# Index scores in rounded parts on 128 rows, decay exponents on ScalarE, two modulation sets in the first network

## The reference

```python
mod = silu(c) @ w_ada + b_ada              # 9 chunks of 2048: the modulation
h = h + 0.5 * g1 * swiglu(mod(rms(h)))     # first network, width 5632
h = h + g2 * mixer(mod(rms(h)))            # 'hn @ w_in', then two branches
h = h + 0.5 * g3 * swiglu(mod(rms(h)))     # second network
# branch 1, state space: 8 groups of 4 heads, causal convolution, softplus dt
seg = acum[:, :, None] - acum[:, None, :]
y_diag = (cc @ bm.T) * exp(where(causal, seg, -inf)) @ x
# branch 2, attention over the 64 keys with the largest index score
rel = relu(einsum('bthd,bsd->bths', q_idx, k_idx))   # 16 heads of 64
score = einsum('bths,bth->bts', rel, w_idx) * idx_scale
```

## Time and profile before

| | us |
|---|---|
| median of 3 runs | 2491.59 |
| lowest, highest | 2489.63, 2493.53 |
| the profiled execution, its own time | 2491.51 |
| its span, first to last instruction | 2489.8 |

### The profile page before, as it was taken

The page is one execution under the profiler, slowest core; times in us unless marked ns, Lnnn a source line. Parts: engine busy times, 40 slices in busy tenths (PEclk is TensorE's granted clock), DMA queues, the critical chain, the costliest instruction groups (busy, mean ns, idle before and its releaser), DMA issues.

```text
span 2489.8 us, 33136 instructions
## 1 busy us (share of the span) xinstructions
PE 2459.8 (99%) x12083; PEld 2075.6 (83%) x12083; DVE 1893.2 (76%) x2168; ACT 1161.6 (47%) x1402; POOL 169.4 (7%) x273
## 2 busy tenths in 40 slices
PE   7999999999999999999999999999999999999999
PEld 5778888888888999898888888888888888888887
DVE  6886679898988989988987777777789555555556
ACT  4444444444446656645556444344544444444443
POOL 4210000000000001111100000000000000000000
PEclk9999999999999999999999999999999999999999
DMA  9975579999986889985544788796698766666665
GB/s 368 375 281 190 193 239 367 312 359 313 361 293 220 270 283 326 305 270 170 181 149 146 270 267 297 254 319 236 236 310 301 221 209 210 210 210 211 211 210 172
DMA packets 290613, 642.78 MB, mean 258 GB/s; under 512 B 26066, under 2 KB 26676, under 8 KB 289588
## 3 DMA queue, kind: packets, MB, share of 16 engines
q1 hardware_dynamic: 269600, 571.41, 67.9%
q0 software_dynamic: 19136, 65.05, 7.9%
q10 hardware_dynamic: 1748, 4.62, 0.5%
HBM read 622.59 MB, written 18.41 MB: 257 GB/s over the span
## 4 chain that ended last, share of the span: by engine, by line
PE 92%; DVE 4%; DMA 2%; ACT 1%; issue 1%; ACTq 0%; DVEq 0%
PE psum L2497 27%; PE psum L2499 27%; PE psum L2498 27%; PE psum L2797 3%; PE psum L2799 3%; PE psum L2798 3%; PE psum L2835 2%; PE psum L2485 1%; DVE w_lo L1541 1%; DMA raw<-in_ffn_w 1%; DVE score L2250 0%; DMA badas<-in_b_ada 0%; PE psum L2539 0%; ACT w_hi L1014 0%; PE psum L2578 0%
## 5 line engine op out<-in xcount | busy, mean ns | idle before, releaser
L1014 ACT ACTIVATE w_hi<-raw 128x1024 fp32r<-128x1024 f32 (+1 forms) x850 | 898.0, 1059 | 1034.0 <-PE psum L2499 819.2
L1541 DVE TENSOR_TENSOR w_lo<-raw,w_hi 128x1024 fp32r<-128x1024 f32 (+1 forms) x850 | 1033.5, 1220 | 448.9 <-ACT w_hi L1014 447.0
L2497 PE MATMUL psum<-w_hi,xT_hi 128*128 128x512 f32 x1984 | 777.6, 392 | 8.1 <-issue 5.4
L2498 PE MATMUL psum<-w_lo,xT_hi 128*128 128x512 f32 x1984 | 773.3, 390 | 0.0
L2499 PE MATMUL psum<-w_hi,xT_lo 128*128 128x512 f32 x1984 | 773.1, 390 | 0.0
L2497 PEld LDWEIGHTS psum<-w_hi,xT_hi 128*128 128x128 f32 x1984 | 373.1, 188 | 91.3 <-issue 14.2
L2499 PEld LDWEIGHTS psum<-w_hi,xT_lo 128*128 128x128 f32 x1984 | 373.0, 188 | 78.5
L2498 PEld LDWEIGHTS psum<-w_lo,xT_hi 128*128 128x128 f32 x1984 | 373.2, 188 | 75.2
L2497 PE MATMUL psum<-w_hi,aT_hi 128*128 128x512 f32 x704 | 274.7, 390 | 0.0
L2499 PE MATMUL psum<-w_hi,aT_lo 128*128 128x512 f32 x704 | 274.0, 389 | 0.0
L2498 PE MATMUL psum<-w_lo,aT_hi 128*128 128x512 f32 x704 | 273.9, 389 | 0.0
(11 more groups left out here) (305 smaller groups left out, 2116.3 us busy)
## 6 DMA issues: line engine op xcount, KB each, us to landing
raw<-in_ffn_w SPq DMA_DIRECT2D x528, 512.0 KB, 4.6
ada_raw<-in_w_ada SPq DMA_DIRECT2D x224, 512.0 KB, 6.3
raw<-in_w_in SPq DMA_DIRECT2D x224, 512.0 KB, 4.5
ada_raw<-in_w_ada POOLq DMA_DIRECT2D x32, 512.0 KB, 6.9
ada_more<-in_w_ada POOLq DMA_DIRECT2D x32, 512.0 KB, 7.4
raw<-in_w_br_ssd SPq DMA_DIRECT2D x32, 512.0 KB, 5.1
raw<-in_w_br_att SPq DMA_DIRECT2D x32, 512.0 KB, 4.6
raw<-in_w_out SPq DMA_DIRECT2D x32, 512.0 KB, 5.1
```

Of the source, the lines that this page charges most:

```text
L1014: nc.scalar.activation(w_hi[:, n.slot(SPLIT), 0:size], raw[:, n.slot(RAW), 0:size], ACT.Copy).then_inc(hi_ready, 1)
L1541: nc.vector.tensor_tensor(w_lo[:, n.slot(SPLIT), 0:size], raw[:, n.slot(RAW), 0:size], w_hi[:, n.slot(SPLIT), 0:size], ALU.subtract).then_ ...
L2497: nc.tensor.matmul(o, hi[:, kt + k, toks], whi, start=a, stop=False)
L2498: nc.tensor.matmul(o, hi[:, kt + k, toks], wlo, start=False, stop=False)
```

## The change

Queries and keys of the index are split into a rounded high and a low part. `qs[0]` holds even heads' high part on rows 0 to 63 and their low part on rows 64 to 127, `qs[1]` the odd heads' the other way round; a product is then two rounded ones on all 128 rows, against `kiT_hi` and `kiT_lo`. ScalarE writes the high parts, VectorE the low ones. The decay's exponents become relu(a - b) on ScalarE, with the exponential of minus that; `acum` loses its sign. Two modulation sets move from the mixer to the units from 43 on of the first network, and the one left in the mixer lies in its steps 40 to 71. `k_lo` moves one step ahead. Some semaphores are merged (`c_turned`, `c_ready`, `h_loaded`, `k_lo_ready`, `q_lo_ready`, `v_hi_ready` into neighbours, with their counts adjusted), and `fold_s` grows to 8 sets; those lines are left out here.

```diff
@@ -57,7 +57,7 @@
-ADA_PEELED = (0, 2)
+ADA_PEELED = (2, 2)
@@ -67,7 +67,7 @@
-ADA_MIXED = 3
+ADA_MIXED = 1
@@ -224,7 +224,9 @@
     cT = place("cT", at_temp + 60 * KB, [GROUPS, T])
-    qiT = place("qiT", at_temp + 68 * KB, [IDX_H // 2, T])
+    qs = (place("qs0", at_temp + 68 * KB, [IDX_H // 2, T], F32R), place("qs1", at_h, [IDX_H // 2, T], F32R))
+    kiT_hi = place("kiT_hi", at_temp + 12 * KB, [T], F32R)
+    kiT_lo = place("kiT_lo", at_temp + 13 * KB, [T], F32R)
     oT_hi = place("oT_hi", at_temp + 52 * KB, [KT, T], F32R)
@@ -674,7 +673,7 @@
 
-        return LATE[f] + (i * 5 // 4 if f == 0 else i * 5 // 3)
+        return LATE[f] + (i * 2 if f == 0 else i * 5 // 3)
 
@@ -694,7 +693,7 @@
                    for i in range(ADA_MIXED) for k in range(KT + ADA_COLS // FOLD_COLS)]
-    MIXED_AT = dict(zip([w for w in range(UPB + 6, 16 * UPB) if light(w)], MIXED_STEPS))
+    MIXED_AT = dict(zip([w for w in range(5 * UPB, 14 * UPB) if light(w)], MIXED_STEPS))
     assert len(MIXED_AT) == len(MIXED_STEPS)
@@ -796,7 +795,7 @@
                         if g >= 2:
-                            sp.wait_ge(seg_ready, g - 1)
+                            sp.wait_ge(seg_bent, g - 1)
                         sp.dma_start(cum_spread[:, g % 2], cum_dram[4 * g:4 * g + 4, :].rearrange("(o r) n -> o r n", o=1)
@@ -1323,17 +1322,22 @@
             act.wait_ge(unit_done, end[b])
-            for j in range(2):
-                ins = nc.scalar.activation(qiT[:, 4 * i + 2 * j:4 * i + 2 * j + 2, :],
-                                           psum[:, pair(b) + j, :].rearrange("p (k t) -> p k t", k=2), ACT.Copy)
-            ins.then_inc(pair_read[b % 2], 1)
+            for e in range(2):
+                own = slice(64 * e, 64 * e + 64)
+                ins = nc.scalar.activation(qs[e][own, 4 * i:4 * i + 4, :],
+                                           psum[own, pair(b):pair(b) + 2, :].rearrange("p b (k t) -> p (b k) t", k=2), ACT.Copy)
+            ins.then_inc(index_hi, 1)
+
+        def ki_out():
+            act.wait_ge(ada_used, ADA_MERGE * KT)
+            nc.scalar.activation(kiT_hi[:], kiT[:], ACT.Copy).then_inc(index_hi, 1)
 
...
@@ -1378,9 +1382,21 @@
 
+        def ssd_segments(g):
+
+            act.wait_ge(cum_in[g % 2], 16 * (g // 2 + 1))
+            act.wait_ge(acum_ready, 1)
+            if g:
+                act.wait_ge(y_raw, g)
+            for half in range(HALF):
+                for k in range(4):
+                    ins = nc.scalar.activation(decay[:, 2 * half, k, :], cum_spread[:, g % 2, k, half * P:(half + 1) * P],
+                                               ACT.Relu, scale=-1.0, bias=acum[:, half, 4 * g + k:4 * g + k + 1])
+            ins.then_inc(seg_bent, 1)
+
         def decay_exp(g):
-            act.wait_ge(seg_ready, g + 1)
-            nc.scalar.activation(decay[:, 0:3:2], decay[:, 0:3:2], ACT.Exp).then_inc(decay_ready, 1)
+            act.wait_ge(seg_bent, g + 1)
+            nc.scalar.activation(decay[:, 0:3:2], decay[:, 0:3:2], ACT.Exp, scale=-1.0).then_inc(decay_ready, 1)
 
@@ -1453,6 +1469,8 @@
                             qi_out(b)
+                            if WBLOCKS[b][1] == 0:
+                                ki_out()
                         if kind[b] == "v":
@@ -1474,6 +1492,8 @@
                     s = ssd_start[g]
+                    if n == s + 2:
+                        ssd_segments(g)
                     if n == s + 3:
@@ -1662,11 +1682,12 @@
                 e, k = divmod(peeled[f], KT)
+                second = e == ADA_PEELED[f] - 1
                 e += (ADA_FIRST, ADA_FFN2)[f]
                 ada_add(At(e * KT + k), k)
-                if e == N_ADA - 1 and 1 <= k <= ADA_COLS // FOLD_COLS:
+                if second and 1 <= k <= ADA_COLS // FOLD_COLS:
                     fold(At(e - 1), (k - 1,))
-                if e == N_ADA - 1 and k == KT - 1:
+                if second and k == KT - 1:
                     fold(At(e))
@@ -1852,6 +1873,7 @@
             sub_units(n + 1)
+            ada_peeled(0)
             if n - 3 == at_unit["w3", 0, 7]:
@@ -2111,28 +2133,20 @@
-            dt_do(nc.vector.tensor_scalar(acum[:, 0:2, :], psum[:, 4, 0:64].rearrange("p (s n) -> p s n", s=2),
-                                          -1.0, None, ALU.mult))
+            dt_do(nc.vector.tensor_copy(acum[:, 0:2, :], psum[:, 4, 0:64].rearrange("p (s n) -> p s n", s=2)))
...
-            nc.vector.tensor_tensor(acum[:, 2, :], psum[:, 4, 64:96], acum[:, 0, :], ALU.add).then_inc(acum_ready, 1)
+            nc.vector.tensor_tensor(acum[:, 2, :], psum[:, 4, 64:96], acum[:, 0, :], ALU.subtract).then_inc(acum_ready, 1)
...
-        def ssd_segments(g):
-
-
-            dve.wait_ge(cum_in[g % 2], 16 * (g // 2 + 1))
-            dve.wait_ge(acum_ready, 1)
+        def ssd_masks(g):
+
...
-            for half in range(HALF):
-                for k in range(4):
-                    nc.vector.tensor_scalar(decay[:, 2 * half, k, :], cum_spread[:, g % 2, k, half * P:(half + 1) * P],
-                                            acum[:, half, 4 * g + k:4 * g + k + 1], 0.0, ALU.add, ALU.min)
@@ -2214,27 +2228,41 @@
...
+
+        def qi_lo(b):
+            i = WBLOCKS[b][1]
+            dve.wait_ge(index_hi, (1, 3)[i])
+            for e in range(2):
+                own, other = slice(64 * e, 64 * e + 64), slice(64 - 64 * e, 128 - 64 * e)
+                ins = nc.vector.tensor_tensor(qs[e][other, 4 * i:4 * i + 4, :],
+                                              psum[own, pair(b):pair(b) + 2, :].rearrange("p b (k t) -> p (b k) t", k=2),
+                                              qs[e][own, 4 * i:4 * i + 4, :], ALU.subtract)
+            ins.then_inc(pair_read[b % 2], 1)
+
+        def ki_low():
+            dve.wait_ge(index_hi, 2)
+            nc.vector.tensor_tensor(kiT_lo[:], kiT[:], kiT_hi[:], ALU.subtract)
@@ -2379,6 +2407,10 @@
                         v_lo(b)
+                    if kind[b] == "qi" and n == end[b] + 3:
+                        qi_lo(b)
+                        if WBLOCKS[b][1] == 0:
+                            ki_low()
                 if n == FRONT_END + 5:
@@ -2390,7 +2422,7 @@
                     if n == s + 2:
-                        ssd_segments(g)
+                        ssd_masks(g)
                     if n == s + 4:
@@ -2409,7 +2441,6 @@
                     top_out()
-                if n == s + 15:
                     k_lo()
@@ -2871,13 +2902,13 @@
                 pe.wait_ge(pair_read[qb % 2], qb // 2 + 1)
-                pe.wait_ge(kiT_ready, 1)
             else:
...
                 for e in range(2):
-                    rows = slice(64 * e, 64 * e + 64)
-                    ins = plain(psum[:, 5 + e, half * T:(half + 1) * T], qiT[rows, j, half * P:(half + 1) * P], kiT[rows, :])
+                    o, both = psum[:, 5 + e, half * T:(half + 1) * T], qs[e][:, j, half * P:(half + 1) * P]
+                    plain(o, both, kiT_hi[:], True, False)
+                    ins = plain(o, both, kiT_lo[:], False, True)
             ins.then_inc(index_done, 1)
```

More of the change, by code:

```diff
@@ L176, in build @@
     dta = place("dta", region(HALF * SSD_H * 4), [HALF, SSD_H])
-    fold_s = place("fold_s", base[0], [6, ADA_COLS // FOLD])
+    fold_s = place("fold_s", base[0], [8, ADA_COLS // FOLD])
     sp_v = place("sp_v", region(HALF * SSD_H * 4), [HALF, SSD_H])
@@ L368, in build @@
     kiT_ready = sem("kiT_ready")
+    index_hi = sem("index_hi")
     dt_step = sem("dt_step")
@@ L381, in build @@
     seg_ready = sem("seg_ready")
+    seg_bent = sem("seg_bent")
     decay_ready = sem("decay_ready")
@@ L404, in build @@
     head_ready = sem("head_ready")
-    k_lo_ready = sem("k_lo_ready")
-    q_lo_ready = sem("q_lo_ready")
-    v_hi_ready = sem("v_hi_ready")
+    head_lo = sem("head_lo")
     p_lo_ready = sem("p_lo_ready")
@@ L989, in _ @@
         act.dma_start(c_row[0:KT, :], c[0].rearrange("(r n) -> r n", n=P)).then_inc(c_in, 16)
-        act.wait_ge(c_ready, 1)
+        act.wait_ge(cols_ready, 1)
         nc.scalar.activation(cact[:], vecT[:, 0:KT], ACT.Silu).then_inc(cact_ready, 1)
@@ L1335, in v_out @@
                 ins = nc.scalar.activation(vt_hi[:, half, :], psum[:, pair(b) + half, :], ACT.Copy)
-            ins.then_inc(v_hi_ready, 1)
+            ins.then_inc(head_ready, 1)
         def head_squares(i, b):
@@ L1520, in mixer @@
             merged_hi(mT2_hi, 0)
-            act.dma_start(h[:], h_dram).then_inc(h_loaded, 16)
+            act.dma_start(h[:], h_dram).then_inc(h_spilled, 16)
             cast_units(n + 6)
@@ L1607, in _ @@
         nc.vector.memset(fold_tmp[:], 0.0).then_inc(fold_step, 1)
-        dve.wait_ge(c_turned, 1)
-        nc.vector.tensor_copy(vecT[:, 0:KT], psum[:, 1, 0:KT]).then_inc(c_ready, 1)
+        dve.wait_ge(rows_turned, 1)
+        nc.vector.tensor_copy(vecT[:, 0:KT], psum[:, 1, 0:KT]).then_inc(cols_ready, 1)
         def columns():
-            dve.wait_ge(rows_turned, 1)
+            dve.wait_ge(rows_turned, 2)
```

(24 more changed lines are left out.)

3 lines of the change are left out of this document (removed).

## The result

The changed kernel took 2496.28 us (median of 18 runs, 2493.88 to 2501.56) beside 2491.40 for the kernel before (18 runs, 2488.94 to 2493.86). The ratio is 1.0024 with a 95% interval of 1.0018 to 1.0030, so it is slower by 4.5 to 7.5 us (the two medians alone are 4.9 apart). The forecast was 2496.2. The profiled execution has a span of 2493.7 us, 3.9 longer than before.

A forecast was written before the change was run, and what follows sets the result against it. TensorE was taken as the bound, busy in all but 30 us. From 2491.59: -2.4 (index) + 5.7 (wait) + 2.4 (clock) - 1.2 (late VectorE) + 0.1 (ScalarE) = +4.6, giving 2496.2 us, range 2492.5 to 2499.5.

The forecast's parts named there:

- The wait: Before the first index product near 1130, TensorE waits 5.7 us (5.0 to 6.6) for `qi_lo` from VectorE.
- The clock: Behind that wait the clock drops to its lower level and charges 2.4 us, bounds 0 and 3.5.
- rival 2: Same wait, but the low clock lasts longer than near the start; passes +5.0 once the clock costs 2.8; chance 0.41.
- The index steps: Eight index products on TensorE, each 0.95 us long, gain 0.31 a step, taken as 2.4 us in all.
- Late VectorE: TensorE's waits for VectorE's low parts at 1211 to 1221 shrink: gain 1.2 us (0 to 1.7), 0.5 left.
- the 1.73 us that was called the most to be had: Three late matmul starts at 1211.7, 1217.7 and 1221.0; moving VectorE work can give back 1.73 us and no more.
- the place at 826: Called the largest other place of the low parts' 2.7 us in five, behind twelve convolution steps the change leaves alone.
- The moved sets: Modulation sets moved from mixer to first network, about 175 to 345 us: cost nothing; if cover failed, 1 to 3 us.
- `k_lo` one step earlier change[s] no order that anyone waits for: Claim that the merged semaphores and the earlier `k_lo` make nobody wait; it had no term in the sum.
- the extra 0.1 that did not show: Term of +0.1 us in the sum for ScalarE's extra work elsewhere.
- rival 1: The forecast itself: wait and clock nearly paid for, time within 0.2% of the kernel before; chance 0.45.
- Rivals 3 and 4: 3: the clock doesn't fall, or hardly, 2493.8 us, chance 0.09. 4: the wait is hidden, 2488.0 us, chance 0.05.

The follow-up runs named there:

- e6b_lo_early: The changed kernel with the index queries' low part (`qi_lo`) one step earlier in VectorE's program: 2490.15 us, ratio 0.9999 to the kernel before.
- e2_no_relu: The changed kernel with the decay's exponents back on VectorE: 2495.64 us, ratio 1.0021 to the kernel before.
- e5b_kept_busy: The changed kernel with 26 matmuls that nobody reads ahead of the first index step's wait: 2494.65 us, ratio 1.0019 to the kernel before.
- e7b_k_back: The changed kernel with `k_lo` back at its old step and with its own semaphore: 2495.64 us, ratio 1.0021 to the kernel before.
- e4_sets_alone: The kernel before with only the two modulation sets moved to the first network: 2490.28 us, ratio 1.0003 to the kernel before.
- e8b_all_three: The changed kernel with `qi_lo` one step earlier, the first index step one unit later and `k_lo` back: 2488.19 us, ratio 0.9988 to the kernel before.
- e3_relu_alone: The kernel before with only the decay's exponents moved to ScalarE: 2489.61 us, ratio 0.9993 to the kernel before.

## Why the prediction was right

**The wait: mechanism and place right, 0.44 us too short.** Forecast 5.7, measured 6.14. The copies took 2.08 where 1.9 was counted, the relus 2.35 (2.3), the cast to `sub` 1.07 (1.10), `sub` and the two subtractions 3.72 (3.5), the signal 0.14 (0). One step of the count is added wrongly: 1132.2 + 3.5 is 1135.7, not 1135.8, so its own terms give a wait of 5.6 and a sum of +4.5. e6b_lo_early, which takes relus, cast and `sub` out of the chain, has 1.3 us of wait, and e2_no_relu, without the relus, 3.6: these three make most of it, not the subtractions. The relus' 0.29 us each was worked out from a spacing with a scalar column. The Trainium skill, "ScalarE: Activation LUTs", section "What ACT_TABLE_LOAD costs", has 280 ns and 0.833 ns a column for an instruction whose bias is a pointer operand, and an overlap of 93 ns where such instructions follow each other. The estimate from that page is 0.29 us as well, and the trace agrees with 2.35 / 8.

**The clock: 2.4 forecast, 2.06 measured (e5b_kept_busy against after).** It fell as forecast. The estimate took the stretch near the start for five microseconds, but those are only its part that lay on the units: before's granted clock is 0.50 there from 40.7 to 47.5, 6.8 us as well. So rival 2's condition, a low clock that lasts longer than near the start, did not come about; of the 6.8 us 2.4 ran out under the wait, which the prediction did not consider. e7b_k_back has 2.7 for the same stop.

**The index steps: 2.4 forecast, 2.40 measured.** From 1124 to 1190 the unit matmuls move by 5.80, and 6.14 + 2.06 - 5.80 = 2.40; 1.86 of it are the last six steps, 0.31 each. A step takes 0.95 us at full clock, as counted from the earlier trace rows.

**Late VectorE: 1.2 forecast, 1.36 measured.** But the stops were worth more than the 1.73 us that was called the most to be had. At each of the three places the matmul after the late one starts about 0.1 late too (the last at 1222.42, 0.34 behind 1222.08 instead of 0.23), as the prediction counted for the index step and not here: about 2.05 in all. 0.70 of it stayed, where 0.5 was forecast:

```profile
1224.53 0.39 PE L2530 MATMUL psum<-w_hi,xT_lo 128*128 128x512 f32 x1
1225.35 0.50 PE L2528 MATMUL psum<-w_hi,xT_hi 128*128 128x512 f32 x1 [0.44 <-DVE w_lo L1561]
1225.69 0.39 PE L2529 MATMUL psum<-w_lo,xT_hi 128*128 128x512 f32 x1
```

The prediction also misread where the 2.7 us of the earlier trace rows lie. 1.22 and 0.24 of them are idle time at 129.7 and 172, and the place at 826 is not among the five. The argument doesn't hang on it. e2_no_relu shows the other side: without the relus' move the index steps' gain is eaten there.

**The moved sets: nothing forecast, nothing measured** (e4_sets_alone, 0.2 us). VectorE was put at about 156 us busy between 175 and 345 and is at 147.7: durations of instructions that overlap a little had been added up. The DMA share was put at 0.91 and is 0.83.

**The step that failed: "`k_lo` one step earlier change[s] no order that anyone waits for".** It cost 0.95 us at 1236, shown by the changed kernel's wait and by its absence in e7b_k_back. VectorE does 2.3 us of work (`kT_lo` and the `sub` behind it) ahead of `qT_lo`, and TensorE's turns stand right behind that. e7b_k_back takes back the place and the merged signal together; the turns start 0.15 us behind the end of `qT_lo`, which is what they wait for in either kernel, so it is the place in VectorE's order that costs.

**The sum.** 6.14 + 2.06 - 2.40 - 1.36 + 0.95 = +5.4, and -0.3 in the rest of the span, gives the table's +5.1; forecast +4.6. The misses in the wait (+0.44) and `k_lo` (+0.95) were covered in part by the clock (-0.34), VectorE (-0.16), the extra 0.1 that did not show, and the -0.3. That the median came out within 0.1 us of the forecast is luck: the ratio allows 4.5 to 7.5 us, and misses of 0.4 and 0.95 were made up by others. Rivals 1 and 2 are one mechanism cut at 5 us, and the interval straddles that line; the clock's price, on which they were to differ, was rival 1's in the changed kernel's trace (2.06) and all but rival 2's in e7b_k_back's (2.7 of 2.8). Rivals 3 and 4 are out: the clock fell, and the wait was not hidden.

## What to carry to other kernels

A product made cheaper on the bounding engine is worth its saving only if its new operands are signalled in time: count from the block's end through every instruction ahead of the signal in each engine's order, those of other edits too, to the place where the bounding engine asks. A stop of several microseconds on TensorE can cost more than itself, because the matmuls behind it run at the lower clock (both stops of 6 us did, shorter ones did or didn't, last section); filling it, or better, moving the asker or the signal by one step, is a one-line edit. And any instruction moved within an engine's order is a term of the sum, however small it looks: one step earlier for `k_lo` cost as much as three index steps gained.

## What the runs showed of the hardware

The same stop of 5.99 us brought a low-clock stretch of about 6.8 us twice, but it began 2.4 us ahead of the end of the stop in one trace and 1.0 in the other, and cost 2.1 and 2.7 us. A stop of 3.65 us brought a stretch of 3.4; one of 1.31 brought none.

The length of a stop alone does not decide this. At the wait for `aT_lo`, 1.92 us in e8b_all_three were followed by 3.4 us of low clock, and 1.69 and 1.61 at the same place in e3_relu_alone and e7b_k_back by none:

```profile
452.30 0.59 PE L2530 MATMUL psum<-w_hi,aT_hi 128*128 128x512 f32 x1 [1.92 <-DVE aT_lo L1838]
...
453.54 0.63 PE L2530 MATMUL psum<-w_hi,aT_hi 128*128 128x512 f32 x1
453.97 0.63 PE L2531 MATMUL psum<-w_lo,aT_hi 128*128 128x512 f32 x1
```

Near 69.8 us e2_no_relu and e4_sets_alone both stop for 2.31 us at the same matmul. These are the windows behind it, first of e2_no_relu, then of e4_sets_alone, with 8 matmuls in the first and 14 in the second:

```profile
70.00:73.00 3.00, 3.00 (x8) 2.33 (x8) 1.54 (x3) 1.06 (x1) 0.72 (x1) 0.50 1.04 385
```

```profile
70.00:73.00 3.00, 3.00 (x14) 2.46 (x14) 1.52 (x3) 1.06 (x1) 0.72 (x1) 1.00 1.05 391
```

Behind the first 20 us, the longest stop without a fall is 2.76 us, in e3_relu_alone up to 144.2. So a stop of about 2 us may or may not bring the low clock, and nothing here says which it will be.

Copies of 64 partitions by 1024 columns took 1.02 us each (two in 2.05) and the subtractions 1.22, where instructions of 128 partitions by 1024 columns take 1.04 and 1.22: half the rows save nothing.

The stretch ahead of the index scatters. By the same matching the traces lie between 3.3 us ahead of before and 1.0 behind it at 195 us, and from 402 to 606 us e3_relu_alone and e7b_k_back lose a further 1.9 to 2.0 and e8b_all_three 3.8. The wait for `aT_lo` is 1.6 to 1.9 of it in each, and in e8b_all_three the low clock behind that wait is another 1.7. The clock has a part in the start too: between 37 and 50 us it is low for 6.8 us in the traces of before, after and e5b_kept_busy, for 3.4 in six others and not at all in e4_sets_alone. I found nothing in the edits that says why the waits differ. All this is as much as the whole change moves, so single spans can't be compared; only the same stretch of two traces, or many runs, can.
